# Small transfers ahead of slot loads, half of the gates' mixing on another engine, and fewer warming products, in a two-block sequence kernel

## Time and profile before

| | us |
|---|---|
| median of 3 runs (2402.49, 2411.49, 2414.29) | 2411.49 |
| span of the profiled execution | 2398.5 |
| time of its own for that execution, beside its span | not given by the page |
| PE busy | 2187.9 (91%) |
| VectorE / ScalarE / GpSimd busy | 1012.5 / 528.5 / 322.0 |
| HBM read | 340.36 MB, 149 GB/s over the span |

### The profile page before, as it was taken

The page is one execution under the profiler, slowest core; times in us unless marked ns, Lnnn a source line. Parts: engine busy times, 40 slices in busy tenths (PEclk is TensorE's granted clock), DMA queues, the critical chain, the costliest instruction groups (busy, mean ns, idle before and its releaser), DMA issues. The chain is left out here.

```text
span 2398.5 us, 39431 instructions
## 1 busy us (share of the span) xinstructions
PE 2187.9 (91%) x16610; PEld 1619.8 (68%) x16610; DVE 1012.5 (42%) x2272; ACT 528.5 (22%) x937; POOL 322.0 (13%) x534
## 2 busy tenths in 40 slices
PE   5998997999999999999997889998998899879988
PEld 3887886787888785788863355565566666436656
DVE  4633532533430473488044344434434441240362
ACT  1112121311000101100022243424423422010251
POOL 0000000000000300000004734433422120000100
PEclk8998998999999999999998889999998899899999
DMA  8643336537864320687215755545544242212200
GB/s 343 227 180 138 141 123 200 112 128 287 303 259 145 136 88 8 233 330 289 106 44 216 236 140 157 156 117 142 162 107 111 50 136 98 82 75 89 87 1 18
DMA packets 127130, 359.73 MB, mean 150 GB/s; under 512 B 78696, under 2 KB 87144, under 8 KB 109424
## 3 DMA queue, kind: packets, MB, share of 16 engines
q1 hardware_dynamic: 93776, 209.90, 25.6%
q0 software_dynamic: 32608, 146.31, 18.0%
q10 hardware_dynamic: 576, 1.05, 0.1%
HBM read 340.36 MB, written 16.85 MB: 149 GB/s over the span
## 5 line engine op out<-in xcount | busy, mean ns | idle before, releaser
L306 PE MATMUL bank<-h,ring 128*128 128x256 f32 x2304 | 498.5, 379 | 5.1 <-DVEq L1111 3.3
L306 PEld LDWEIGHTS bank<-h,ring 128*128 128x128 f32 x2304 | 437.3, 190 | 68.1 <-DVEq L1111 4.9
L1956 PE MATMUL bank<-rw_feed 128*128 128x512 f32 x464 | 251.8, 653 | 16.0 <-ACT rkv L2161 6.5
L1743 POOL DMA_DIRECT2D rw_feed<-rwkv_mixes x232 | 124.5, 537 | 475.5 <-PE bank L1956 469.6
L2270 DVE TENSOR_TENSOR rw_u<-bank,rw_lam 128x128 f32<-128x128 f32 x120 | 34.9, 291 | 301.5 <-PE bank L1875 295.8
L1021 PE MATMUL bank<-ffn_hidden,ring 128*128 128x256 f32 x704 | 152.4, 379 | 3.4 <-PEq L1047 3.4
L525 PE MATMUL bank<-h,ring 128*128 128x256 f32 x640 | 145.8, 385 | 8.4 <-PEq L323 8.4
L1021 PEld LDWEIGHTS bank<-ffn_hidden,ring 128*128 128x128 f32 x704 | 133.6, 190 | 22.2 <-issue 4.1
L525 PEld LDWEIGHTS bank<-h,ring 128*128 128x128 f32 x640 | 122.1, 193 | 28.3 <-issue 12.1
L139 PE MATMUL bank<-con 128*128 128x512 f32 x236 | 109.6, 616 | 32.3 <-DVE mod L133 14.4
L1956 PEld LDWEIGHTS bank<-rw_feed 128*128 128x128 f32 x464 | 78.3, 197 | 87.3 <-issue 47.7
(11 more groups left out here) (432 smaller groups left out, 3375.9 us busy)
## 6 DMA issues: line engine op xcount, KB each, us to landing
ring<-in_stream SPq DMA_DIRECT2D x79, 2048.0 KB, 8.0
rw_feed<-rwkv_mixes POOLq DMA_DIRECT2D x232, 256.0 KB, 3.2
next_w<-in_mod_stream POOLq DMA_DIRECT2D x24, 2048.0 KB, 9.9
ctx<-in_mod_rest POOLq DMA_DIRECT2D x16, 1024.0 KB, 6.3
rw_feed<-in_rkvg POOLq DMA_DIRECT2D x232, 64.0 KB, 3.4
rwkv_mixes<-mixed SPq DMA_DIRECT2D x8, 1024.0 KB, 3.9
y<-bias_table SPq DMA_DIRECT2D x48, 128.0 KB, 4.9
rw_at<-rw_at_kept SPq DMA_DIRECT2D x16, 256.0 KB, 4.3
```

The source lines that it names most:

```text
L306: mm = pe.matmul(out, ring_tile(k, n, kt, i * P), rhs[kt], start=start and kt == kts[0], stop=stop and kt == kts[-1])
L1743: pool.dma_start(feed[:, g % FEED, 0:512], mixes[j, :, g % KT, :]).then_inc(fed[g % FEED], 16)
L1956: pe.matmul(k.psum[PROJ], feed[:, g % FEED, 512:], feed[:, g % FEED, 0:512], start=(kt == 0), stop=(kt == KT - 1)).then_inc(eaten, 1)
```

## The change

- Opening: 6 warming products instead of 14.
- hyin: SP loads two slots ahead, then waits for the masked bias and stores it, then loads the other eight.
- ssm: SP loads seven slots ahead, then the 18 bias tiles, then the last three slots.
- rwkv_in: the gates' mixture is made by ScalarE and GpSimd for tiles 0 to 3 and by VectorE, behind v, for tiles 4 to 7. The lora weights of the first head pair and the scan's four tables are loaded here, the tables after the first lora product is up, and not in the scan. The buffer of r lies in the slots' ring, and `w2`, `sel` and `half2` are allocated before the stage.
- scan: SP's list starts with the spills.

```diff
@@ stage_opening, tensor
             pe.wait_ge(k.slot_used, first + RING - 1)
-            keep_warm(k, pe, 7, 14)
+            keep_warm(k, pe, 7, 6)
@@ stage_hyin, sync
-            load_ahead(k, sp, first, NFIRST)
+            load_ahead(k, sp, first, 2)
             sp.wait_ge(bias_masked, 1)
             sp.dma_start(table.ap(), flat[:]).then_inc(bias_kept, 16)
+            load_ahead(k, sp, first + 2, NFIRST - 2)
             sp.wait_ge(bias_kept, 16)
@@ stage_ssm, sync
-            load_ahead(k, sp, first, NT // 4)
+            load_ahead(k, sp, first, NT // 4 - 3)
             sp.wait_ge(gated, 4)
             for i in range(3):
                 load_bias(sp, y, table, bias_landed, i)
+            load_ahead(k, sp, first + NT // 4 - 3, 3)
@@
+def scan_tables(k):
+
+    return k.par[:, 0:512], const(k, "tri")[:, 0:64]
@@ stage_rwkv_in
-        bufs = [sb(f"mixed{i}", KT, 512) for i in range(4)]
+        in_ring = k.ring[:].rearrange("p r s -> p (r s)")[:, 3 * D:3 * D + KT * 512].rearrange("p (k t) -> p k t", k=KT)
+        bufs = [sb(f"mixed{i}", KT, 512) for i in range(3)] + [in_ring]
...
@@ stage_rwkv_in, sync
             sp.dma_start(w0, a["rkvg"][0:3, 0].rearrange("j p c m -> p j c m")).then_inc(w0_landed, 16)
+            sp.dma_start(w2, a["lora_out"][:, :, 0:P]).then_inc(k.w2_landed, 16)
+            starts, gmask = scan_tables(k)
+            sp.wait_ge(lora_up, 1)
+            for dst, src in ((half2, "half_masks"), (sel[0:8, :], "head_sel"), (starts, "chunk_starts"), (gmask, "gram_mask")):
+                sp.dma_start(dst, a[src]).then_inc(k.tables_landed, 16)
             for j in (K, R, V, G):
                 for half in range(2):
                     at = slice(HALF * half, HALF * half + HALF)
-                    sp.wait_ge(mixed[j], HALF * (half + 1))
+                    if j == G and half:
+                        sp.wait_ge(gates_mixed, HALF)
+                    else:
+                        sp.wait_ge(mixed[j], HALF * (half + 1))
                     sp.dma_start(mixes[j, :, at, :], place[j][:, at, :]).then_inc(dumped, 16)
@@ stage_rwkv_in, gpsimd
-            for kt in range(KT):
+            for kt in range(HALF):
                 pool.wait_ge(scaled, kt + 1)
                 nc.gpsimd.tensor_tensor(place[G][:, kt, :], place[G][:, kt, :], h[:, kt, :], ALU.add).then_inc(mixed[G], 1)
@@ stage_rwkv_in, vector
+            dve.wait_ge(lora_up, 2)
+            for kt in range(HALF, KT):
+                mix(G, kt).then_inc(gates_mixed, 1)
@@ stage_rwkv_scan, sync
-            load(0)
-            sp.dma_start(half2, a["half_masks"]).then_inc(consts, 16)
-            sp.dma_start(sel[0:8, :], a["head_sel"]).then_inc(consts, 16)
-            sp.dma_start(starts, a["chunk_starts"]).then_inc(consts, 16)
-            sp.dma_start(gmask, a["gram_mask"]).then_inc(consts, 16)
             for dst, src in zip(x_kept, (k.x, k.ctx)):
                 sp.dma_start(dst.ap(), src[:].rearrange("p a t -> p (a t)")).then_inc(spilled, 16)
@@ stage_rwkv_scan, tensor
-            pe.wait_ge(consts, 64)
+            pe.wait_ge(k.tables_landed, 64)
...
```

More of the change, by code:

```diff
@@ L1340, in mod2, with stage_rwkv_in @@
     return k.next_mod[:, int(ctx), c:c + 8]
-def stage_rwkv_in(nc, k, a, h, lora, rkv, mixes):
+def scan_tables(k):
+    return k.par[:, 0:512], const(k, "tri")[:, 0:64]
+def stage_rwkv_in(nc, k, a, h, lora, rkv, mixes, w2, sel, half2):
     R, K, V, G, W, A = range(6)
@@ L1361, in stage_rwkv_in @@
         dumped, scaled = sem("mix_dumped"), sem("mix_scaled")
-        w0_landed = sem("w0_landed")
+        w0_landed, gates_mixed = sem("w0_landed"), sem("gates_mixed")
         place = {W: bufs[0], A: bufs[1], K: bufs[2], R: bufs[3], V: bufs[0], G: bufs[1]}
@@ L1530, in scan_order, with stage_rwkv_scan @@
     return order
-def stage_rwkv_scan(nc, k, a, lora, rkv, mixes, xa, o):
+def stage_rwkv_scan(nc, k, a, lora, rkv, mixes, xa, o, w2, sel, half2):
     HALF_E = -math.exp(-0.5)
@@ L1585, in stage_rwkv_scan @@
         ATb, Xb, outer = sb("at", LCH, LCH), sb("x", LCH // 2, LCH), sb("outer", 144)
-        w2 = sb("w2", 2, P)
         kk, lwr, av = sb("kk", 512), sb("lwr", 2, 512), sb("av", 2, 512)
@@ L1597, in stage_rwkv_scan @@
         wout += [dead[:, 2048:3072], ATb.rearrange("p s t -> p (s t)")]
-        starts, gmask, sel, half2 = k.par[:, 0:512], const(k, "tri")[:, 0:64], sb("sel", 512), sb("half2", 6)
+        starts, gmask = scan_tables(k)
         cen, omka, eps = const(k, "neg"), sb("omka", KT), sb("eps", 1)
@@ L1605, in stage_rwkv_scan @@
         x_kept = [nc.dram_tensor(f"rw_{s}_kept", (P, KT * T), F32) for s in ("x", "ctx")]
-        consts, step, inits = sem("consts"), sem("step"), sem("inits")
+        step, inits = sem("step"), sem("inits")
         spilled, back, o_out = sem("spilled"), sem("back"), sem("o_out")
         o_kept = nc.dram_tensor("rw_o_kept", (P, 4, 512), F32).ap()
-        loaded, at_out, at_in, x_out, mt_in = (sem(n) for n in ("loaded", "at_out", "at_in", "x_out", "mt_in"))
+        at_out, at_in, x_out, mt_in = (sem(n) for n in ("at_out", "at_in", "x_out", "mt_in"))
         fed = [k.by_pool[f"fed{b}"] for b in range(FEED)]
@@ L1670, in load @@
             def load(n):
-                if n >= 1:
-                    sp.wait_ge(lora_up, 2 * n)
-                sp.dma_start(w2, a["lora_out"][:, :, n * P:(n + 1) * P]).then_inc(loaded, 16)
+                sp.wait_ge(lora_up, 2 * n)
+                sp.dma_start(w2, a["lora_out"][:, :, n * P:(n + 1) * P]).then_inc(k.w2_landed, 16)
             def blocks(t, n, d, h):
@@ L1779, in lora_products @@
                 if j == 0:
-                    pe.wait_ge(loaded, 16 * (n + 1))
+                    pe.wait_ge(k.w2_landed, 16 * (n + 1))
                 outs = [take("lora", n, j, d) for d in range(2)]
@@ L2184, in _ @@
             v.scalar_tensor_tensor(cen, headones, -1.0 / 64, ident, ALU.mult, ALU.add).then_inc(inits, 1)
-            dve.wait_ge(consts, 64)
+            dve.wait_ge(k.tables_landed, 64)
             def elements(n, d):
@@ L2411, in second_block @@
         rkv = lay.enter_context(nc.sbuf_tensor("rkv", [P, 2, 3, 512], F32))
+        w2 = lay.enter_context(nc.sbuf_tensor("rw_w2", [P, 2, P], F32))[:]
+        sel = lay.enter_context(nc.sbuf_tensor("rw_sel", [P, 512], F32))[:]
+        half2 = lay.enter_context(nc.sbuf_tensor("rw_half2", [P, 6], F32))[:]
         with nc.sbuf_tensor("h_both", [P, KT, 512], F32) as h:
             stage_turnover(nc, k, h)
-            stage_rwkv_in(nc, k, a, h, lora, rkv, mixes)
+            stage_rwkv_in(nc, k, a, h, lora, rkv, mixes, w2, sel, half2)
         o = lay.enter_context(nc.sbuf_tensor("rwkv_o", [P, 4, 512], F32))
         xa = lay.enter_context(nc.sbuf_tensor("rw_xa", [P, 4, 1536], F32))
-        stage_rwkv_scan(nc, k, a, lora, rkv, mixes, xa, o)
+        stage_rwkv_scan(nc, k, a, lora, rkv, mixes, xa, o, w2, sel, half2)
     stage_mla(nc, k, a)
@@ L2775, in build @@
         k.w1_landed = top.enter_context(nc.semaphore("lora_in_landed"))
+        k.w2_landed = top.enter_context(nc.semaphore("lora_out_landed"))
+        k.tables_landed = top.enter_context(nc.semaphore("scan_tables_landed"))
         k.by_pool = {n: top.enter_context(nc.semaphore(n)) for n in (
```

## The result

Four runs of the changed kernel had a median of 2365.26 us (2364.3 to 2383.86), four of the kernel before 2407.7 (2402.49 to 2414.29). The ratio is 0.9846, 95% interval 0.9818 to 0.9874: 37 us faster, between 30 and 44 (the two medians themselves lie 42 us apart). The forecast was 2379.8, in a range of 2365 to 2397, so the median lies 0.3 us inside its lower end. The profiled execution's span fell from 2398.5 to 2363.6 us, where the sum said 2366.8.

A forecast was written before the change was run, and what follows sets the result against it. TensorE, busy in 91% of the span, was taken to lose time to idling at stage ends, low clock and warming; five terms summed to 31.7 us, span 2398.5 to 2366.8, plus 13.0 gives 2379.8, range 2365 to 2397.

The forecast's parts named there:

- Opening: Opening: warming is the stage's end; six products instead of 14 end at 42.05, gain 6.9 us.
- Hyin's end: Hyin to ssm: PE starts 7.2 us earlier, but the head table lands late behind a slot load; term 4.0 us.
- Clock cover and charge: Opening: PE's 7 us of work covers the clock; ssm's new wait: 1.3 us charged for a 1.2 GHz stretch.
- Ssm's end: Ssm to attention: 14.5 us at the boundary, plus 2 for attention's clock, minus 2 for delayed pieces; term 14.5.
- it repeats at the next piece: Ssm's end: the bias loads' delay, repeating at VectorE's next modulation piece, costs 3.5 to 6.5 us; 2 taken.
- The sum that went with the rule: Ssm's end: if queues alternate packet by packet, pieces lose almost nothing; sum 2 us better, 2378.
- Gates' mixing: Gates' mixing stage: both dumps go out together after GpSimd, the second landing 0.4 us later than now; term -0.4.
- I keep that distance: Whole kernel: the runs' median stays 13.0 us above the profiled span, so 2366.8 becomes 2379.8.
- A: Rival, whole kernel: every term lands at its better end; 41.7 us gained, time 2370; chance 0.14.
- B: Rival, whole kernel: collisions at their bad ends, the pieces above all; 22.2 us gained, time 2389; chance 0.14.
- D: Rival, stage ends: another late engine just behind the removed one; 15 us gained, time 2396; chance 0.04.
- C: Rival, scan: TensorE's clock falls more from the new start; near 2405 or 2424; chance 0.08, half slower, half unchanged.

The follow-up runs named there:

- table_late: The changed kernel with the bias table's store behind all ten slot loads of hyin again; one run of 2390.52 us.
- the repeat: The changed kernel once more, unaltered, against the kernel before; 2374.68 us, ratio 0.9877 (0.9844 to 0.9911).
- only_bias_tiles: The kernel before with only the 18 bias loads moved ahead of ssm's last three slot loads; 2396.74 us, ratio 0.9951 to the kernel before.
- head_early: The changed kernel with ssm's small head table loaded in hyin, before its slot loads; 2366.09 us, ratio 0.9833 to the kernel before.
- gates_undo: The changed kernel with all eight tiles of the gates on ScalarE and GpSimd again; one run of 2364.67 us.

## Why the prediction was right

**Opening**: 6.9 forecast, 6.2 and 6.6 in two traces. Right; six products took 7.99 and 7.60 us instead of 7.3. Hyin's first product came at 44.23 and not near 42.3, mostly as warming began 1.2 us later, behind a clock that rose later; it began at 34.7 to 36.4 in the traces, with the change and without.

**Hyin's end**: 4.0 forecast, 3.8 to 4.3 measured. The step that mattered, that the table's store had hidden the head table's load, is shown by three kernels. The table was expected 11 us after hyin's last product (203 against 192.04) and was used 11.6 after it (201.95 against 190.35); the turn waited 5.45 us where 6 were named. Clock cover and charge were of the right size: table_late gains 5.1 at the turn and 4.0 to 4.3 at ssm's end.

**Ssm's end**: 14.5 forecast, 17.0 measured. The 14.5 at the boundary were right (15.48 - 0.93), and the 2 for attention's clock came as 2.5 (6.73 - 4.26). The wrong term is the 2 charged for VectorE's pieces. The collision happened: the first wait went from 5.49 to 10.37 us. But the step "it repeats at the next piece" failed: the three waits are 22.4 us in sum before and 22.1 after (5.49 + 7.46 + 9.46; 10.37 + 5.54 + 6.23). The second piece went out at 371.8 before, with a slot load in the engines until 374.9; it goes out at 371.2 now, and that load lands at 372.6. The third went out 2.1 us behind the next slot load before, and goes out 5.1 us behind it now. That nothing of the charge is left in this trace is partly luck, though. Over the eleven traces with this edit the three waits are 21.9 to 24.9 us in sum, 23.3 in the mean, against 22.4 and 22.2 in the two of the kernel before, and the idle at this boundary is 0.93 to 2.84 us. So some 1 us is the charge, where 2 was taken.

The first piece's 5 us have two parts. These are the packets of the changed kernel's queues (q1 is SyncE's, q0 GpSimd's; number, MB, share of the engines) at 358.3 to 361.6 us, 361.6 to 364.5 and 364.5 to 368.4; the piece was issued at 358.29:

```profile
q1 hardware_dynamic: 407, 0.37, 100.0%
...
q0 software_dynamic: 102, 0.84, 69.1%
q1 hardware_dynamic: 76, 0.06, 30.0%
...
q1 hardware_dynamic: 104, 1.53, 91.8%
q0 software_dynamic: 42, 0.21, 13.1%
```

In the first 3.4 us no packet of the piece moved, only bias packets (2.6 us in the repeat, 1.9 in only_bias_tiles); before, its first came 1.2 us after its issue. Then the two queues took turns, and from 364.5 on the eighth slot load shared the engines with its end, where before it came behind the piece. The Trainium skill (DMA: Bandwidth & Descriptors, Queues, rings and completion order) says that an engine takes turns between its queues packet by packet, from which the prediction took that the piece would lose almost nothing to the small bias packets. The middle rows agree with the turns; the price does not agree, for 2.2 us went before the piece's first packet (0.7 to 1.4 in the other two traces). In only_bias_tiles the wait was as long (10.87). Why the piece began so late is not shown. The sum that went with the rule, 2 better, came nearer, but by another way.

**Gates' mixing**: -0.4 forecast, -0.3 measured, and its mechanism is shown by three kernels. The last dump landed 6.5 us after GpSimd's end, as named (1270.9 + 6.0 against 1269.2 + 1.25).

**Scan's opening**: 6.7 forecast, 6.6 measured; the spills' possible price wasn't seen.

**The span and the median.** The span came at 2363.6 for 2366.8. That it is so near is partly luck: the rows forecast at nothing (-3.3, -1.5 and 7.4) and the 1.2 us of the opening nearly cancel. The median then came 14.5 us below the forecast, by the step "I keep that distance". The 13.0 us between the median and the span aren't something that every run has. Where the profiled run's own time is known the distance is small: 2417.7 over 2416.0, 2390.52 over 2388.8, 2356.97 over 2355.3, always 1.7. The first trace was by this of a run of about 2400.2 us, which lay below all three runs shown; the other 11 us are scatter, of the scan above all. With them the median nearly left the range, although the sum was right. The ratio's own gain (37 and 29.6 us) lies on either side of 31.7.

**The rivals.** A had three of its parts wrong (the head table, overlapping dumps, a clock without falls); its time, 2370, is nearer to the median than the forecast is, for reasons that aren't its own. B is refuted by ssm's end. D found no late engine: TensorE idles for 1.15 and 0.93 us at two of the ends, and the scan's first product comes 1.33 us into its stage. C was right that the scan's clock can move. That the new start decides it isn't shown: with no edit at all the scan moves by 6 to 13 us, and the six runs of head_early alone lie 24 us apart. The ten traces whose kernels hold most of the change have 118 us of low clock in the mean, the three others 134; at 0.45 that would be 7 us for the change, but with a spread of 92 to 150 three traces can't settle it.

The 1.5 us lost between ssm's out product and the mixing stage are no part of the change: from the out products' end on it is 716.0 us before and 717.4 in both traces of the change, but 715.8 in gates_undo and 715.9 in head_early. What stays open is what sets off the fall in hyin.

## What to carry over

At a stage's end ask not only which wait is removed but which small transfer was issued in its shadow: here some 3 of 7 us went to a 32 KB load that had cost little until then, and moving that load as well gave them back, and more. In this kernel a small transfer belonged ahead of the large one on its queue as soon as its data was ready, and dumps in the order in which their data was finished. Read such a change by stretches between two landmarks that both traces have, and take no term smaller than the scatter (here some 10 us, in the scan) from whole times.

## What was not expected of the hardware

- A 32 KB load took 10.5 us behind a 2 MB load, and 1.6 (table_late) to 3.4 us (the kernel before) in empty engines.
- Eighteen 128 KB loads took 13.96 us of issuing. A 1 MB load of another queue, issued 1.1 us after the last of them, landed 5 us later than before, 2.2 us of it before its first packet.
- TensorE's clock rose in the opening's sum of squares at 18.1 to 21.4 us, in the same code, and the 16 records took 5.1 to 6.7 us by it.
- One GpSimd add of 1.25 us stood for 13.72 us while VectorE ran its mixes back to back (some 19 of them, 0.67 us each); it got no turn between two of them.
- The clock fell within hyin's products, where TensorE is busy without a pause, for 6.8 us in ten of thirteen traces, 3.4 in one and not at all in two, the kernel before being on both sides. In the changed kernel it began 17.4 us after the first product, while the narrow products of 32 columns ran.
